# Expert layers of a diffusion backbone: each expert scattered alone through 32-row products, gate and up products ahead of the preceding down products, nine and ten weight slots

## The reference

```
h   = modulate(rms_norm(x, g_ffn[l]), sh2, sc2)
aff = softmax(h @ w_router, axis=-1)               # (N tokens, 16 experts)
gate, idx = top_k(swapaxes(aff, 1, 2), cap)        # cap = 2*N/16 = 32 tokens an expert
xe  = h[idx]                                       # (16, 32, 1024)
a   = einsum("ecd,edf->ecf", xe, w_gate)           # w_*: 16 x 1024 x 1024
u   = einsum("ecd,edf->ecf", xe, w_up)
ye  = einsum("ecf,efd->ecd", silu(a) * u, w_down) * gate
x   = x + gt2 * zeros.at[idx].add(ye)
```

## Time and profile before

| | |
|---|---|
| median of 3 runs | 1949.43 us (1948.41 to 1950.66) |
| profiled execution | 1948.21 us |
| its span | 1945.2 us |
| PE busy | 1693.5 us (87%), 10298 instructions |
| DVE, ACT, POOL busy | 729.5, 490.2, 121.1 us |
| HBM read | 540.84 MB, 280 GB/s over the span |
| mean granted TensorE clock | 0.962 |

### The profile page before, as it was taken

How to read it: one execution, slowest core, us unless ns; L and a number is a source line. 1 busy time by engine, 2 the same in 40 slices (tenths; PEclk the granted TensorE clock), 3 DMA queues, 4 the chain that set the end, 5 groups by cost and what they waited for, 6 DMA issues and landing times.

```text
span 1945.2 us, 25261 instructions
## 1 busy us (share of the span) xinstructions
PE 1693.5 (87%) x10298; PEld 988.6 (51%) x10298; DVE 729.5 (38%) x1611; ACT 490.2 (25%) x1063; POOL 121.1 (6%) x175
## 2 busy tenths in 40 slices
PE   5999999988998999999898799988898987687765
PEld 2887777765665333333332498866693322222221
DVE  3356666564434112121211556766553110101102
ACT  4225554551123000000000435554341000000000
POOL 1002210000001000000000101300001000000000
PEclk9999999998999999999999899989899999898998
DMA  9332221126677999999999543345579999999996
GB/s 351 119 97 81 88 81 61 33 76 203 234 296 295 386 428 428 427 428 427 428 428 418 187 141 111 104 145 194 164 293 383 427 427 427 428 427 429 426 428 262
DMA packets 147772, 545.44 MB, mean 280 GB/s; under 512 B 9482, under 2 KB 91600, under 8 KB 123084
## 3 DMA queue, kind: packets, MB, share of 16 engines
q1 hardware_dynamic: 145260, 537.68, 70.3%
q0 software_dynamic: 2400, 6.16, 1.1%
HBM read 540.84 MB, written 2.98 MB: 280 GB/s over the span
## 4 chain that ended last, share of the span: by engine, by line
PE 50%; DMA 26%; DVE 13%; ACT 6%; issue 4%; SPq 0%; DVEq 0%; POOL 0%; ACTq 0%
PE bank L1893 18%; DMA ring<-in_w_exp_down 10%; PE bank L1761 7%; PE bank L1762 7%; PE bank L1763 7%; DMA ring<-in_w_exp_up 7%; DMA ring<-in_w_exp_gate 6%; DVE WL L1371 3%; PE bank L1943 2%; PE bank L1675 2%; PE bank L1871 2%; ACT WH L1139 2%; DMA ring<-in_w_in 2%; ACT PB L1223 1%; DMA ring<-in_w_ada 1%
## 5 line engine op out<-in xcount | busy, mean ns | idle before, releaser
L1893 PE MATMUL bank<-ring,XEP 128*32 128x256 f32 (+1 forms) x3072 | 466.8, 619 | 59.1 <-DMA ring<-in_w_exp_gate 35.4
L1893 PEld LDWEIGHTS bank<-ring,XEP 128*32 128x32 f32 (+1 forms) x3072 | 143.4, 129 | 371.1 <-issue 289.8
L1761 PE MATMUL bank<-HH,WH 128*128 128x512 f32 (+1 forms) x864 | 310.3, 359 | 9.3 <-DVE WL L1371 4.3
L1762 PE MATMUL bank<-HL,WH 128*128 128x512 f32 (+1 forms) x864 | 304.1, 352 | 0.0
L1763 PE MATMUL bank<-HH,WL 128*128 128x512 f32 (+1 forms) x864 | 302.9, 351 | 0.0
L1371 DVE TENSOR_TENSOR WL<-ring,WH 128x1024 fp32r<-128x1024 f32 (+1 forms) x172 | 185.0, 1076 | 180.0 <-ACT WH L1139 179.3
L1893 PE MATMUL bank<-ring,HIDT 128*32 128x256 f32 (+1 forms) x1536 | 184.7, 477 | 42.2 <-DMA ring<-in_w_exp_down 28.3
L1761 PEld LDWEIGHTS bank<-HH,WH 128*128 128x128 f32 x864 | 166.9, 193 | 45.0 <-issue 15.1
L1139 ACT CAST WH<-ring 128x1024 fp32r<-128x1024 f32 (+1 forms) x172 | 158.5, 925 | 123.0 <-PE bank L1763 60.5
L1763 PEld LDWEIGHTS bank<-HH,WL 128*128 128x128 f32 x864 | 167.0, 193 | 21.7
L1762 PEld LDWEIGHTS bank<-HL,WH 128*128 128x128 f32 x864 | 167.4, 194 | 20.3
(11 more groups left out here) (214 smaller groups left out, 1869.7 us busy)
## 6 DMA issues: line engine op xcount, KB each, us to landing
ring<-in_w_exp_gate SPq DMA_DIRECT2D x64, 2048.0 KB, 28.2
ring<-in_w_exp_up SPq DMA_DIRECT2D x64, 2048.0 KB, 28.5
ring<-in_w_exp_down SPq DMA_DIRECT2D x64, 2048.0 KB, 29.7
ring<-in_w_ada SPq DMA_DIRECT2D x48, 1024.0 KB, 7.4
ring<-in_w_in SPq DMA_DIRECT2D x40, 1024.0 KB, 5.5
ring<-in_w_in SPq DMA_DIRECT2D x28, 512.0 KB, 5.1
ring<-in_w_branch SPq DMA_DIRECT2D x24, 512.0 KB, 6.2
ring<-in_w_out SPq DMA_DIRECT2D x4, 2048.0 KB, 8.5
```

The lines of the kernel that those rows point to most:

```text
L1761: mm(t, wh, hi[:, k, 0:b.n], start=k == 0, stop=False)
L1762: mm(t, wh, lo[:, k, 0:b.n], start=False, stop=False)
L1893: last = mm(out_bank[tw * c:tw * c + tw, 0:nw], stationary(k), w[:, c::G] if spread else w[:, nw * c:nw * c + nw], start=k == 0, stop=k == ...
```

## The change

Every expert now scatters alone. Its four blocks of 32 rows and 512 columns (layer 0: two halves of the output times two sets of tokens) or 32 rows and 256 columns (layer 1: four quarters) stay on the partitions on which `YAB` has them, so that `YE` is one operation and each scatter matmul contracts 32 rows, at `tile_position` (32i, 0). The scatter of expert e - 2 is cut into four pieces, put behind the 2nd, 4th, 6th and 8th of the eight contraction steps of expert e's gate product; that of expert 14 goes into the last down product, that of 15 follows, into eight (four) banks of its own. The down product of expert e - 1 comes behind the up product of expert e, and has the turning of e's hidden values in its middle. Selection tables are made by VectorE, an expert or a pair at a time (`weigh`, `pick`), and `SELT` is gone. The slots become nine in layer 0 (`split_slot`, where the split mixing weights were) and ten in layer 1 (also `spare`, the context halves of `X` and `MRG`). In layer 1 chunk 0 is loaded at the start of the mixing stage (behind `ht_ready`), chunk 1 behind the gt2 bias, and three instead of four wait for `dense_done`. The last chunk of a layer comes in four pieces. `GT2` holds one block of columns a group of rows, so its bias is 256 KB in layer 0 and 128 KB in layer 1, and one selection product instead of two finishes each half of it in layer 0. The output is written by two DMAs.

```diff
-NSLOT = 8
-ORDER = [[2, 3, 6, 7, 4, 5, 0, 1], [3, 6, 7, 4, 5, 0, 1, 2]]
+ORDER = [[2, 3, 6, 7, 4, 5, 8, 0, 1], [9, 4, 3, 6, 7, 5, 8, 0, 1, 2]]
+NSL = [len(o) for o in ORDER]
+GATE_AT = [0] + [6 * e - 2 for e in range(1, NE)]
+UP_AT = [c + 2 for c in GATE_AT]
+DOWN_AT = [6 * e + 8 for e in range(NE - 1)] + [NCH - 2]
...
+        if last:
+            expert_load(Step(o_ready=("ht_ready", 2 * KD)))
         ch = col_chunk("nv")
...
                 P.add("gt2_bias", l=l, sets=P.sets)
+                if last:
+                    expert_load(Step(o_ready=("pv_ready", P.sets)))
...
-            for _ in range(4):
+            for _ in range(3):
                 expert_load(dense_done)
...
-                        for c in range(NSLOT, NCH):
-                            sp.wait_ge(chunk_used, NCH * l + c - NSLOT + 1)
+                        for c in range(NSL[l], NCH):
+                            sp.wait_ge(chunk_used, NCH * l + c - NSL[l] + 1)
                             load_expert(l, c)
...
+                        def add_rows(e):
+                            e0, a0 = NE * l + e, add0 + adds * e
+                            dve.wait_ge(chunk_used, NCH * l + DOWN_AT[e] + 2)
+                            nc.vector.tensor_tensor(YE[:, 0:nw], YAB[:, 0:nw], GT2[:, 0:nw], ALU.mult).then_inc(ye_ready, 1)
...
+                            for i, (tile, c) in enumerate(parts):
+                                dve.wait_ge(sc_ready, a0 + i + 1)
...
+                                nc.vector.tensor_tensor(xs, xs, ys, ALU.add).then_inc(x_added, 1)
...
+                        def scatter(e, first, n):
+                            e0, a0, banks, ends = NE * l + e, add0 + adds * e, scatter_banks(e, s.ns), e == NE - 1
+                            if first == 0:
+                                pe.wait_ge(ye_ready, e0 + 1)
+                                pe.wait_ge(stb_ready, e0 + 1)
+                            for i in range(first, first + n):
+                                if not ends and a0 + i > 1:
+                                    pe.wait_ge(x_added, a0 + i - 1)
+                                elif ends and i == 0:
+                                    pe.wait_ge(x_added, a0)
+                                if s.ns == 2:
+                                    j, q, c = i // 4, i // 2 % 2, i % 2
+                                    rows = slice(64 * c + 32 * q, 64 * c + 32 * q + 32)
+                                    last = mm(banks[i][:], STB[e % 2][rows, 128 * j:128 * j + 128], YE[rows, :], start=True, stop=True,
+                                              tile_position=(64 * c + 32 * q, 0))
...
+                                last.then_inc(sc_ready, 1)
...
+                            product(GAB, chosen(e), GATE_AT[e], G == 4, e // 2 if e % 2 == 0 else None, scatter_between(e - 2) if e > 1 else None)
+                            if e % 2 == 0 and n < NPAIR:
+                                gather(n)
+                            product(UAB, chosen(e), UP_AT[e], G == 4)
+                            if e % 2 == 0 and n < NPAIR:
+                                turn_rows(n)
+                            if e:
+                                down(e - 1, lambda k: turn_hidden(e) if k == 3 else None)
+                            else:
+                                turn_hidden(e)
+                            turn_gates(e)
+                        down(NE - 1, scatter_between(NE - 2))
+                        scatter(NE - 1, 0, adds)
```

More of the change, by code:

```diff
@@ L50, with last_in_slot @@
 SH1, SC1, GT1, SH2, SC2, GT2V = range(6)
+def last_in_slot(l, i):
+    return NCH * l + max(c for c in range(NCH) if c % NSL[l] == i) + 1
 def shape_constants():
@@ L320, in turn @@
             def turn():
[L321 to L324, removed]
+                s.out = [P.tile(dve=True) for _ in range(2 if v == SC2 else 1)]
+                if v != GT2V:
                     P.mods += len(s.out)
@@ L562, in make_plan @@
         dense_done = Step(used_tile=stage_c_end)
[L563 to L567, removed]
+        late = []
         P.add("router_load", c_tile=stage_c_end)
         if last:
-            for _ in range(4):
+            for _ in range(3):
                 expert_load(dense_done)
@@ L624, in make_plan @@
         P.add("route", ns=ns, l=l, early=late, lt=lt, at=at, code=P.tile(dve=True))
-        for c in range(len(early), NSLOT):
+        for c in range(len(early), NSL[l]):
             j = ORDER[l][c]
@@ L632, in make_plan @@
                   c_tile=stage_c_end, d_tile=dense_end, recent=list(P.recent), act=P.act, dve=P.dve)
-        P.occupants = [(SLOT * j, SLOT * (j + 1), Step(expert=l, slot=ORDER[l].index(j))) for j in range(NSLOT)]
+        P.occupants = [(SLOT * j, SLOT * (j + 1), Step(expert=l, slot=ORDER[l].index(j))) for j in range(NRING)]
         P.recent = [None] * NBLK
@@ L1895, in product @@
+                                w = expert_row(l, c, k % 4)
+                                for g in range(G):
+                                    last = mm(out_bank[tw * g:tw * g + tw, 0:nw], stationary(k), w[:, g::G] if spread else w[:, nw * g:nw * g + nw],
+                                              start=k == 0, stop=k == KD - 1, tile_position=(0, tw * g))
                                 if k % 4 == 3:
                                     last.then_inc(chunk_used, 1)
+                                if between:
+                                    between(k)
@@ new lines, in chosen, with hidden, scatter_between, turn_hidden @@
+                        def chosen(e):
+                            return lambda k: xep[e // 2 % 2][:, e % 2, s.ns * k:s.ns * k + s.ns, :].rearrange("p a t -> p (a t)")
+                        def hidden(e):
+                            return lambda k: HIDT[e % 2][:, k, 0:tw]
+                        def scatter_between(e):
+                            step = 2 if s.ns == 2 else 1
+                            return lambda k: scatter(e, step * (k // 2), step) if k % 2 else None
+                        def turn_hidden(e):
+                            e0 = NE * l + e
+                            pe.wait_ge(hid_ready, e0 + 1)
+                            if e0:
+                                pe.wait_ge(stb_ready, e0)
+                            for c in range(8 // G):
+                                cols = slice(c, 512, 4) if G == 2 else slice(128 * c, 128 * c + 128)
+                                last = nc.tensor.transpose(HTB[:, 128 * c:128 * c + 128], HID[:, cols], IDENT)
+                            last.then_inc(hid_turned, 1)
@@ new lines, in turn_gates, with down @@
+                        def turn_gates(e):
+                            e0 = NE * l + e
+                            pe.wait_ge(hidt_ready, e0 + 1)
+                            pe.wait_ge(selg_ready, e0 + 1)
+                            for j in range(2):
+                                last = nc.tensor.transpose(HTB[:, 128 * j:128 * j + 128], SELG[:, j, :], IDENT)
+                            last.then_inc(gates_turned, 1)
+                        def down(e, between=None):
+                            if NE * l + e:
+                                pe.wait_ge(ye_ready, NE * l + e)
+                            product(YAB, hidden(e), DOWN_AT[e], False, between=between)
```

309 lines of the change are left out of this document (152 added, 157 removed).

## The result

The changed kernel takes **1957.53 us** (median of 9 runs, 1954.41 to 1964.68) against 1949.43 us before, measured beside it (9 runs, 1942.04 to 1952.36). The ratio is 1.0048 with a 95% interval of 1.0035 to 1.0062: about half a per cent slower. The forecast was 1952.4 with a range of 1935 to 1979, and slower was its likeliest side at 0.47. The profiled execution took 1957.53 us with a span of 1955.5, 10.3 us more than before.

What follows compares the result with a forecast made beforehand. TensorE was taken to bound layer 0's experts, the weight loads layer 1's. 1948.2 + 9.0 (layer 0) - 6.0 (layer 1: -9.2 + 2.5 + 0.7) = 1951.2, and 1.2 from profiled execution to median, gave 1952.4 us, range 1935 to 1979.

Steps and rivals of the forecast that it cites:

- The price of a pair: TensorE time of one inserted pair of scatter matmuls in layer 0, 60 pairs: 1.21 us, bounds 0.86 and 2.07.
- rival 1: Layer 0's insertions: a pair is cheaper than 1.16 us, at 1.0 us the kernel takes 1940 us; chance 0.26.
- rival 2: Layer 0's pairs do not run side by side: 2.07 us each gives 2004 us, 1.64 gives 1978; chance 0.16.
- the forecast's 0.10 us: Part of a pair's price in layer 0: 0.10 us for an exposed weight load.
- Rival 3: Chunk 1 costs layer 1's mixing stage its whole 4.9 us and TensorE waits for adds: 1961 us; chance 0.08.
- Layer 0's experts: Layer 0's expert stage, bound by TensorE: starts at 630.2 us, last add at 1099.9 instead of 1090.0.
- +9.0: Layer 0 in all: +9.9 us at the last add, -0.9 for one selection product fewer in the mixing stage.
- The forecast's floor by the loads: Layer 0 if only the loads bound it: end at 1077.5 us, a floor of -12.5 us.
- -9.2: Start of layer 1's weight stream: one chunk earlier, 4.9 us, and 4.3 us of start gap covered by two more slots.
- +2.5: Layer 1's mixing stage: chunk 1 ahead of the mixing weights adds 4.9 us, the smaller bias saves 2 to 3.
- +0.7: Layer 1's tail: about 3 us gained by smaller last pieces, against interleaved scatter delaying the last steps and later final squares.

Runs made afterwards that it cites:

- e1: Changed kernel with the two scatter matmuls of each layer 0 pair on the same 32 rows instead of two row groups: 2012.35 us, ratio 1.0325.
- e6: Changed kernel with each expert's down product back behind its own gate and up products, in both layers: 1964.04 us, ratio 1.0083.
- e2: Changed kernel with layer 0's scatter in two insertions of four matmuls on four row groups, into four banks: 1937.79 us, ratio 0.9950.
- e4: Changed kernel with layer 1 back to eight slots and no chunk loaded in the mixing stage: 1960.78 us, ratio 1.0052.
- e9: Changed kernel with only layer 1's chunk 1 issued after the projection's weights instead of ahead of the mixing weights: 1949.75 us, ratio 0.9995.
- e7: e5 with layer 1's chunk 1 issued after the projection's weights instead of ahead of the mixing weights: 1920.55 us, ratio 0.9861.
- e3: Changed kernel with expert 14's scatter in layer 1 in one piece ahead of the last down product: 1953.12 us, ratio 1.0017.
- e5: Changed kernel with the edits of e2 and e3, and one insertion of four-row-group matmuls an expert in layer 1: 1934.6 us, ratio 0.9926.
- e8: e5 with eight instead of nine weight slots in layer 0: 1933.66 us, ratio 0.9928.
- e10: e7 with layer 1's four bias rows also issued behind the projection's weights, ahead of chunk 1: 1922.99 us, ratio 0.9865.

## Why the prediction was right, and where not

**The price of a pair** was forecast at 1.21 us from the transitions around the transposes, and is 1.21. That carries the case: rival 1 (1.0 us) and rival 2 (1.64 or 2.07) both fall. Rival 2's upper bound is real, however: e1 made it happen, at 2.05 us, with layer 0 longer by 51.5 us where the text said 52. The total came out; how it divides between the weight load and the two changes of tile form, no run shows. By the Trainium skill (TensorE: Matmul & The Clock Gate, The mechanism) a weight load for other row groups is pulled ahead of running matmuls; by that rule alone the forecast's 0.10 us for it would have gone, and the time would have been 1946 us. A total of 1.21 us does not bear out the 1.11 us that this leaves. Rival 3's adds do not bind: from the first product to 1089 TensorE has no wait for an add. Its other half, that chunk 1 costs the mixing stage its whole 4.9 us, came true and more, as told below.

**Layer 0's experts** were to take 1099.9 - 630.2 = 469.7 us, whenever they start; they take 471.0. Of the 1.3 us, 0.8 is expert 0's wait (3.3 against 2.5). The "+9.0" for layer 0 measured as +8.0, with a start 3.1 us earlier of which 0.9 was forecast; starts scatter by more than that. The stalls of 0.69 and 0.85 us did go with the moved down product; e6 brings them back. The forecast's floor by the loads had a small slip (1066.9 + 10 is 1076.9, not 1077.5); e2 ended the stage at 1076.4.

**Layer 1's stream, "-9.2 and +2.5"**, came out at -4.5 instead of -6.7. From the end of the mixing stage to the last landing it is 495.1 before and 488.0 after, so -7.1 stands for the -9.2 (and e4, with the same bias and scaling as after, says 8.7 for the slots). The +2.5 is 344.6 - 342.0 = +2.6, right as a sum and wrong inside: chunk 1 was priced at 4.9 us, the time that it takes on the queue, and costs 7.4 (e9) to 8.0 (e7), since the mixing weights land 5.8 us later (11.17 against 5.33 us after their issue) and the clock was low behind the longer wait; the smaller bias was priced at "2 to 3" and the stage without the chunk is 4.5 to 5.1 shorter than before (337.5 in e9 and 336.9 in e4 against 342.0), though no run changes the bias alone. Two errors of about the same size cancelled, which is luck. Had the chunk been priced by itself against the trace, the edit that undoes it might have been seen beforehand.

**The tail, "+0.7", is the term that was mis-sized most: it measured +6.9.** The step had the interleaved scatter delay "the last steps by two or three pieces", at their usual price. What it left out is the clock: the granted clock fell to 0.5 at 1926.8, a microsecond behind a wait of 2.70 us, and stayed there. Three more pieces at 1.87 and four insertions at 2.0 us lie where the load was meant to be the last thing; at clock 1.0 they would take 6.5 us less (the estimate above), which is about the 6.2 us missed. In e3, e5, e6, e7, e8 and e10 the scatter is out of that product, and the tail is 14.3 to 15.2 us; in after, e1, e2, e4 and e9 it is in, and the tail is 24.0 to 25.8. The clock goes with it: in those five the granted clock falls to 0.5 for good 2.7 to 4.8 us ahead of the last landing, in the six others only 1.2 to 6.5 us behind it. That the interleave brings the fall is not shown, since no run holds one fixed and changes the other, and a wait alone does not explain it: before's 2.49 us for its last weights brought none. So how the 9 to 10 us between the two groups divide between insertions and clock stays open. The three us that the split last chunk and the smaller scaling were to gain fit the 18.1 before against 15 without the interleave; no run undoes them alone.

Together: forecast by steps was a span of 1951.2 - 3.0 = 1948.2 us. Layer 0's experts took 1.3 more, the stream 2.2, the tail 6.2, and the start 2.3 less, which makes the 1955.5. The median was 5.1 us above the forecast, inside its range, and the likeliest side was the right one. That side owes something to luck. The forecast was 0.15% slower, within what it called no change; with the tail as forecast the time would have been about 1951.3 us, 0.1% above before. What made the kernel clearly slower is the tail, and not the price of a pair, on which the chances were built.

## What to carry to other kernels

Work that is put between the steps of a stream is free only while something else is late; in the last product it is on the path, here at the lower clock too, so it belongs ahead of the wait. An early load must be placed by what stands behind it in the queue: a chunk of 4.9 us cost 7 to 8 ahead of awaited weights, and nothing behind them. Where small matmuls on separate rows run side by side, fill all four groups of rows before adding another insertion: here four cost what two did.

## What the runs showed of the hardware

- Two 32-row matmuls on different rows take 1.13 us, four take 1.14, and two on the same rows 1.98 (float32, 512 columns, each in two records). An insertion between the steps of a product costs 1.21 us with either two or four.
- Granted clock and idle time in the mixing stage: with a wait of 3.1 us (before) it was at 0.5 for 3.4 us from just ahead of the wait's end, with 6.4 us (after) for 6.8 us from the middle of the wait, with 0.2 and 0.3 us (e7, e9) it stayed at 1.0. In the tail of after it fell to 0.5 a microsecond behind a wait of 2.70 and stayed until the end, although products and insertions followed each other without a gap for 13.7 us. In e9 it fell to 0.5 at 1923.2 behind waits of 2.13 and 1.05 us. Before, it stayed at 1.0 behind waits of 2.49 and 1.85 us.
- At 0.5 the products and insertions of layer 1 took 1.87 and 2.0 us instead of 1.0 and 1.05.
